# A decoder block with a top-4-of-32 MoE: the first expert's tokens gathered from three tiles during the routing of the fourth, the fourth tile's added by one-hot products, and the slot table finished inside the first up products

## The reference

```python
x2 = x + mixed @ w_out                       # after the mixers
h  = rms_norm(x2, norm2_g)
logits = h @ router_w + router_b             # 512 x 32
top_v, top_i = lax.top_k(logits, 4); gate = softmax(top_v)
# for each expert e, over the tokens that chose it:
hc  = xb @ w1[e] + b1[e]                     # 1024 -> 2048
gt  = minimum(hc[:, :1024], 7);  up = clip(hc[:, 1024:], -7, 7)
glu = gt * sigmoid(1.702 * gt)
y   = ((up + 1) * glu) @ w2[e] + b2[e]       # 1024 -> 1024
out[token] += gate * y                       # then + x2, final rms_norm
```

## Time and profile before

| | us |
|---|---|
| median of 3 unprofiled runs | 1592.78 (1592.43 to 1592.91) |
| the profiled execution | 1598.76 |
| its span | 1597.1 |
| PE busy in the span | 1535.7 (96%) |
| DVE busy | 512.5 (32%) |
| POOL busy | 313.2 (20%) |
| mean traffic with HBM over the span | 295 GB/s |

### The profile page before, as it was taken

How to read it: one execution, slowest core, us unless ns; L and a number is a source line. 1 busy time by engine, 2 the same in 40 slices (tenths; PEclk the granted TensorE clock), 3 DMA queues, 4 the chain that set the end, 5 groups by cost and what they waited for, 6 DMA issues and landing times.

```text
span 1597.1 us, 31119 instructions
## 1 busy us (share of the span) xinstructions
PE 1535.7 (96%) x12965; PEld 706.4 (44%) x12966; DVE 512.5 (32%) x941; ACT 247.6 (16%) x509; POOL 313.2 (20%) x449
## 2 busy tenths in 40 slices
PE   7999999999999789999999999999999999999992
PEld 4655555665445323334444444444443344344430
DVE  4104555242425433223222422332233223322332
ACT  4212443233412100000100010000001000000001
POOL 2000002341100202212222221222122212121101
PEclk9999999999999799999999999999999999999996
DMA  8122131521261589999999999999999999999985
GB/s 235 27 56 50 40 79 27 168 79 30 66 261 53 219 336 403 407 409 415 416 408 411 416 414 408 413 414 412 408 416 414 412 408 416 415 413 410 413 340 191
DMA packets 108445, 468.15 MB, mean 293 GB/s; under 512 B 29591, under 2 KB 71615, under 8 KB 83794
## 3 DMA queue, kind: packets, MB, share of 16 engines
q1 hardware_dynamic: 94610, 446.55, 69.5%
q0 software_dynamic: 13792, 21.00, 6.0%
HBM read 452.41 MB, written 19.29 MB: 295 GB/s over the span
## 4 chain that ended last, share of the span: by engine, by line
PE 80%; DMA 15%; DVE 2%; issue 1%; ACT 1%; SPq 0%; DVEq 0%; PEld 0%; POOL 0%; ACTq 0%; PEldq 0%; POOLq 0%
PE ps L1613 34%; DMA ring<-in_expert_w 14%; PE ps L1220 12%; PE ps L1631 10%; PE ps L1367 7%; PE ps L1635 5%; PE ps L1556 4%; PE ps L1352 2%; PE ps L1329 2%; PE ps L1339 1%; ACT mixT L1023 1%; PE ps L1508 0%; DMA ring<-x 0%; DMA xs<-in_x 0%; PE ps L1532 0%
## 5 line engine op out<-in xcount | busy, mean ns | idle before, releaser
L1613 PE MATMUL ps<-ring,oT_fox 128*32 128x512 f32 x6144 | 674.4, 596 | 2.9 <-DMA ring<-in_expert_w 2.7
L1613 PEld LDWEIGHTS ps<-ring,oT_fox 128*32 128x32 f32 x6144 | 241.7, 110 | 413.8 <-issue 376.4
L2170 DVE TENSOR_TENSOR mixT<-ps,mask 128x768 f32<-128x768 f32 x64 | 61.0, 952 | 688.1 <-PE ps L1613 688.1
L1631 PE MATMUL ps<-ring,hT 128*32 128x512 f32 x2048 | 276.4, 592 | 1.6 <-DMA ring<-in_expert_w 1.6
L1635 PE MATMUL ps<-ring,hT 128*32 128x256 f32 x2048 | 169.1, 379 | 0.0
L1635 PEld LDWEIGHTS ps<-ring,hT 128*32 128x32 f32 x2048 | 81.7, 110 | 136.7 <-issue 132.3
L1367 PE MATMUL ps<-hT,ring 128*128 128x512 f32 x304 | 137.0, 597 | 0.0
L1147 ACT ACTIVATE mixT<-mixT 128x768 f32<-128x768 f32 x32 | 27.1, 847 | 617.4 <-DVE mixT L2174 598.3
L843 POOL DMA_INDIRECT oT_nsa<-table,pc x93 | 101.1, 1087 | 47.4 <-POOL pc L838 28.0
L1631 PEld LDWEIGHTS ps<-ring,hT 128*32 128x32 f32 x2048 | 78.6, 110 | 35.1 <-DMA ring<-in_expert_w 2.5
L1220 PE MATMUL ps<-hT,ring 128*128 128x512 f32 x208 | 91.7, 601 | 0.0
(11 more groups left out here) (301 smaller groups left out, 1128.3 us busy)
## 6 DMA issues: line engine op xcount, KB each, us to landing
ring<-in_expert_w SPq DMA_DIRECT2D x192, 2048.0 KB
ring<-in_w_in SPq DMA_DIRECT2D x28, 512.0 KB, 4.9
ring<-in_w_out SPq DMA_DIRECT2D x8, 512.0 KB, 9.0
ring<-in_w_in SPq DMA_DIRECT2D x1, 2144.0 KB, 13.3
xs<-in_x SPq DMA_DIRECT2D x4, 512.0 KB, 5.2
ring<-in_w_in SPq DMA_DIRECT2D x8, 256.0 KB, 3.5
ring<-in_w_proj_nsa SPq DMA_DIRECT2D x16, 128.0 KB, 2.8
ring<-in_w_proj_fox SPq DMA_DIRECT2D x8, 256.0 KB, 3.0
```

Of the source, the lines that this page charges most:

```text
L1613: ins = pe.matmul(wide(ps[TG * j:TG * j + TG, g, :]), xT[b][:, g, c, :], up_slab(c, j), start=(c == 0), stop=(c == NK - 1), tile_position= ...
L1631: pe.matmul(ps[TG * q:TG * q + TG, 4, :], gT[b][:, q // 2, c, :], ring[:, NK + j, at:at + 512], start=False, stop=(c == NK - 1), tile_posi ...
L2170: return dve.tensor_tensor(to, half, b_up[:, 256 * n:256 * n + 256].unsqueeze(1).broadcast_to([P, NG, 256]), ALU.add)
```

## The change

The first gather no longer waits for the last tile. After table 2 is filled, DVE takes expert 0's token numbers as they then are (`take_earlier`), and POOL gathers from the first 384 rows of the table; slots that are still empty or out of range are skipped, and a memset of `xg[0]` ahead of it leaves them zero. PE transposes these rows as an accumulation with the identity (`turn_earlier`), four products before and four behind the counting of tile 3. DVE marks expert 0's slots of tile 3 (`mark_first`: the one-hot column times the token's norm factor), and PE adds tile 3's tokens into the same PSUM by `pick_last`, with x2 itself as the weights. Parts 0 to 2 of the last table and `spread_slots` move into up(0), behind chunks 0, 1 and 2. up(0) writes to banks 5 to 7 (`HC_FIRST`). DVE does `take_x(1)` ahead of `expert(0)` rather than inside it. SP issues the two w2 loads of expert 0 first, and stores the last tile behind them.

The core of the diff:

```diff
@@ sync
             sp.wait_ge(out_full, 2 * NT)
-            store_table(NT - 1)
-            sp.wait_ge(xg_loaded[0], 16)
-            store_x2(NT - 1)
             for u in range(NK // 2, 6):
                 load_pair(0, u)
+            sp.wait_ge(table_stored, 16 * NT)
+            store_table(NT - 1)
+            store_x2(NT - 1)
@@ gpsimd
+            pool.wait_ge(mix_full, NK)
+            step.link(pool.memset(xg[0][0:CAP, :], 0.0))
             for t in range(NT):
+                if t == NT - 1:
+                    pool.wait_ge(idx_ready, 1)
+                    pool.wait_ge(table_stored, 16 * NT)
+                    pool.indirect_dma_start(out=xg[0][0:CAP, :], out_offset=None, in_=table_d[0:(NT - 1) * P, :],
+                                            in_offset=bass.IndirectOffsetOnAxis(ap=idx_x[0:CAP, 0:1], axis=0),
+                                            bounds_check=(NT - 1) * P - 1, oob_is_err=False).then_inc(xg_loaded[0], 16)
                 pool.wait_ge(mean_sq, NT + t + 1)
...
-            pool.wait_ge(idx_ready, 1)
-            pool.wait_ge(table_stored, 16 * (NT + 1))
-            pool.indirect_dma_start(out=xg[0][0:CAP, :], out_offset=None, in_=table_d,
...
@@ tensor
+            def turn_earlier(n):
+                every = xg[0][0:CAP, :].rearrange("a (m c) -> a c m", c=NK)
+                for k in range(4 * n, 4 * n + 4):
+                    pe.matmul(first_x(k, k + 1), every[:, k, :], ident[0:CAP, 0:CAP], start=(k % 4 == 0), stop=False,
+                              skip_group_check=True)
+            def pick_last(n):
+                every = xs[:, NT - 1, :].rearrange("p (m c) -> p c m", c=NK)
+                for k in range(4 * n, 4 * n + 4):
+                    ins = pe.matmul(first_x(k, k + 1), every[:, k, :], first_hot, start=False, stop=True, skip_group_check=True)
+                ins.then_inc(xT_full, 1)
             turn_x2(2 * NT - 1)
             route(2 * NT - 1)
+            pe.wait_ge(xg_loaded[0], 16)
+            turn_earlier(0)
             count_earlier(NT - 1)
-            for part in range(len(HOT_PARTS)):
-                fill_table(NT - 1, part)
+            turn_earlier(1)
+            pe.wait_ge(first_marked, 1)
+            pick_last(0)
+            pick_last(1)
...
                 def used(c, ins):
                     ins.then_inc(w1_used, 1)
-                    if isinstance(e, int) and e == 0 and c == 0:
+                    if not before and c == 0:
+                        fill_table(NT - 1, 0)
+                    if not before and c == 1:
+                        fill_table(NT - 1, 1)
+                        fill_table(NT - 1, 2)
+                    if not before and c == 2:
+                        pe.wait_ge(parts_taken, 1)
                         spread_slots()
...
-                if not before:
-                    pe.wait_ge(parts_taken, 1)
-            pe.wait_ge(count_taken, 1)
-            turn_first_x()
@@ vector
+            def mark_first():
+                dve.tensor_scalar(first_hot, slot_no, placed_at[:, NT - 1, 0:1], rs2[:, NT - 1:NT], ALU.is_equal, ALU.mult)\
+                   .then_inc(first_marked, 1)
...
             take_first_x()
+            for part in range(1, len(HOT_PARTS)):
+                mark(NT - 1, part)
+            take_parts()
+            take_quarters()
             weigh(NT - 1)
-            take_quarters()
             count_extra()
-            expert(0, 0, gather)
+            take_x(1, 1, gather)
+            expert(0, 0, None)
```

## The result

| | before | after |
|---|---|---|
| median of 7 runs each, us | 1592.78 (1590.36 to 1593.09) | 1597.43 (1596.37 to 1600.56) |
| the profiled execution, us | 1598.76 | 1596.37 |
| mean granted clock in it | 0.982 | 0.985 |

The account below looks back on a forecast made before the run. PE's loop at 31.47 us an expert was taken as the bound, with up(1)'s start moving the end. Terms -5.1 + 0.5 + 0 = -4.6 us gave 1588.2 us on the median; range 1583.9 to 1592.5.

Parts of the forecast that it names:

- the sentence that the median leaves such waits only 1 us: PE's loop: weight loads cost 7.0 us in the profiled execution, leaving 1591.8; the median 1592.78 thus holds about 1 us.
- Term 1: From the last dense product to up(0): early gather saves 6.5 us, its loaded landing costs 1.4, net -5.1; start 535.1.
- a mild and a severe rival: First gather late at 9.6 us (1590.8), or served only behind both w2 loads (about -0.3 us); together chance 0.14.
- The rival in which the gather is late: First gather, before counting: lands at 9.6 us, 1590.8, or behind both loads, about -0.3 us; no change, together chance 0.14.
- the severe form: First gather served only behind both w2 loads, at 534.5 to 535.5; counting at 536, result about -0.3 us.
- Term 2: From up(0) to up(1): 30.1 us, 0.5 more than before, as take_x(1) waits for expert 1's gather ahead of the clips.
- Term 3: Clock around the start of up(1): falls in the 3.0 us gap, same 2.9 us loss as before, so 0.
- the first rival: Clock stays up between up(0) and up(1): -7.5 us in all, 1585.3, chance 0.2.
- The two other rivals with the clock: Short products hold the clock down in up(0): 1590.8 to 1592.1, chance 0.14; or for longer, 1597.7, chance 0.05.

Follow-up runs that it names:

- the wide products around the routing: Nine unread float32 products of 512 columns added in PE's idle stretches, against the changed kernel with w2 loads behind the gather: 1589.83 us, ratio 0.9980 to before.

## Why the prediction was wrong

**What bounds the kernel.** Right: PE's loop with its period, and up(1) as the start of both PE's and the loads' stream. up(31) comes 5.4 to 7.2 us behind 29 periods in all of them. Wrong was the sentence that the median leaves such waits only 1 us. No trace bears it out. What differs between executions is, for a good part, the clock. Over 85 runs of the kernel before, those with a mean granted clock of 0.982 took 1596.1 us on average, at 0.984 it was 1593.6, at 0.986 it was 1591.3. The profiled execution had 0.982 and 1598.76. Before's runs average 0.9842, the changed kernel's 16 runs 0.9829. At 0.984 on both sides the difference is still 5.0 us (1598.6 of three runs against 1593.6 of 28), at 0.985 it is 3.9 (three against 23), so the loss isn't mainly one of clock.

**Term 1, the start of up(0): the step that failed.** Forecast E + 11.3, came at E + 20.5. In its own terms:

| step | forecast | came | off by |
|---|---|---|---|
| gather lands, behind E | 7.15 | 11.3 | +4.2 |
| `turn_earlier(0)`, to the count | 0.75 | 2.0 | +1.3 |
| counting | 0.41 | 0.3 | -0.1 |
| `turn_earlier(1)` | 0.75 | 2.0 | +1.3 |
| `pick_last` and scaling, to the bias | 2.17 | 4.9 | +2.7 |

In all it is 9.2 us, in which two sizes were off: the landing by 4.2 us and the products by 5.2. The landing: I had the mechanism (the gather shares with the w2 loads, and PE stands before it with the counting behind) and both a mild and a severe rival for it, but took the lowest loaded row, 7.0, and wrote that such gathers take 9.6 us and not longer; here they took 11.1 and 10.9. This one met two loads issued at the same moment (SP at 521.79, POOL at 521.91). The Trainium skill, "DMA: Bandwidth & Descriptors", section "Queues, rings and completion order", has the engines take turns by the packet. The trace agrees with that from 526 on (71 and 56 packets in the same 3 us), not for the 4.5 us ahead, in which the gather moved none. What I didn't do is multiply. My estimate: 7 packets an engine, each behind one of 16 KB, at the 492 GB/s of the earlier trace rows over 16 engines (31 GB/s an engine, 0.53 us a packet) are 3.7 us on 4.3, which makes 8.0. The other 2.7 us of late first packet, which no row of before shows, bring it to 10.7 of the 11.1.

The products: I priced `turn_earlier` and `pick_last` by the transpositions of line 1581, 8 in 1.51 us. Those are one record each. A float32 product of 96 columns is two records and 0.5 us, against 0.19, and this price hardly depends on the clock (see the wide products around the routing). Each record of a `turn_earlier` has a weight load of 0.31 to 0.34 us, where those of line 1581 are 0.19 to 0.23. A nearer row was in the trace of before, and I left it out of the earlier trace rows:

```profile
526.27 1.92 PE L1508 MATMUL ps<-v_sel,oT_fox 128*128 128x32 f32 x8 [0.52 <-DVE oT_fox L2089]
```

These are the four products of `route`: float32, two records each, 0.48 us each at the half clock. The float32 products of 512 columns come as two records each too, 24 for twelve, and I had written that count down.

With the loads behind the gather the kernel is not slower than before (a gain of 0.16%), so the changed kernel as a whole needs both errors to lose; but part of that gain is the order on DVE, as said above. The rival in which the gather is late, and the routing waits for it, had the consequence right. Its landing, 11.3 behind E, is inside the 10.7 to 11.7 (534.5 to 535.5) of the severe form, but that was luck: the severe form has the gather served only behind both loads, and the trace has it beside them. I let that rival end at no change, since it was summed with products at the wrong price.

**Term 2, up(0) to up(1).** Forecast 30.1 us, came 28.9. The length of up(0), forecast 25.5, was 25.6 to the start of `fill_gates`. DVE did wait for expert 1's gather, as forecast, but that landed 6.2 us behind its third issue (559.25 to 565.44), better than the 6.8 that I took. That it came near was partly luck. I had read the 0.25 MB by 557 as expert 1's tokens, but by then POOL had issued three more gathers, for expert 2; in the kernels before with take_x first the same tokens landed 8.1 and 7.9 us behind the third issue. The clips follow at once, and the gap was 1.73 and not 3.0.

**Term 3, the clock.** The fall ahead of up(1) came as forecast, and the first rival (it stays up) was wrong for this kernel, though not for the shorter variants. But the same loss as before it was not: of the low stretch (3.4 us in place of 6.8) 3.2 us lie behind the start of up(1) in place of 5.9, so 1.4 us less. In the profiled executions the terms close: -4.6 + 9.2 - 1.2 - 1.4 = +2.0, which is where up(2) came, behind E. The two other rivals with the clock, short products in up(0), didn't happen.

**What stays open.** The runs lost 4.7 to 5.4 us, the profiled executions 2.0 behind E. The mean clocks (0.982 in before's profiled execution against 0.984 over its runs, 0.985 in after's against 0.983) have the sign and about the size (2.6 us between 0.982 and 0.984 over the runs of before), but the unprofiled executions have no trace to show where. Open is also why the first packet of the gather came 4.5 us behind its issue.

## What to carry to other kernels

Before you issue a small gather that an engine waits for, look at what the same moment puts into the other queues: order the large loads behind it by a wait on its semaphore if they have slack, as the w2 loads had here. Price a new product by a row of the same kind (product or transposition, data type, records per product, length of its weight load), not by the row that stands at the same place. Run each part of a change alone: here one moved line, the order on DVE, gave 4.7 to 5.8 us by itself, and no version with the early gather can be told from it as faster. Where a gap ahead of dense work is closed, count the clock as well as the gap, and check the mean granted clock of the profiled execution against those of the runs before its time is taken as typical.

## What the runs showed of the hardware

- One gather of 96 rows of 4 KB, of which only part is moved (0.26 MB, 112 packets), took 4.3 us alone, 8.9 us with one 2 MB load issued beside it, 11.1 and 10.9 us with two. Its first packet moved 4.5 us after the issue, with one load or two, in place of 1.8; from there on it took 2.0, 3.7 and 6.2 us.
- A float32 product of 96 columns took 0.50 us at the half clock (8 in 4.03) and about as much at the full one (4 in 1.92 and 2.12); a transposition of the same data took 0.19 (8 in 1.51, half clock).
- In the kernel with the loads behind the gather PE was busy with products of 96 and 32 columns from 526.2 to 534.5 without a gap, at 0.50; the clock rose at 539.7, 4.0 us into chunk 0. In the four kernels with two to six wide products in the gap ahead of up(1), it didn't fall there in the profiled execution. Of eight kernels without them and with a gap of 1.7 to 1.9 us, it fell in five (in one of them 1.1 us behind the gap) and not in the other three, so the gap's length alone doesn't tell.
- The stretch of low clock around the start of up(1) lasted 3.4 us in four profiled executions, 6.8 in three and was missing in seven. up(1) to up(2) took 34.7 us with the long one and 31.7 without. Over the 85 runs of before, which spread over 8.4 us, the average falls by 4.9 us from a mean clock of 0.982 to 0.986; where the clock was low in them no trace shows.
